# Heads with one difference and two products per halving, and feed-forward products over both parts of the operand at once

## The chip, the cores and the metric

The kernel runs on one core of a Trainium2 chip. The metric is the device time of one execution, in microseconds (us); the same program is executed several times and the median is compared. Matrices are float32 and every large product is made of three products of rounded parts, described below.

## The reference

Two blocks in a row on a sequence of 256 tokens, width 2048. Cut to what the change touches:

```python
# first block, end: feed-forward with a squared relu, 2048 -> 8192 -> 2048
h = x * (1.0 + sc2) + sh2
f = jnp.square(jax.nn.relu(h @ w_m1[l] + b_m1[l])) @ w_m2[l] + b_m2[l]
x = layer_norm(DEEPNORM_ALPHA * x + g2 * f, ln2_g[l], ln2_b[l])
...
# second block, layer 1: gated linear recurrence, 16 heads of 128, forward and backward
b = jnp.cumsum(fb, axis=2)                      # running sum of log forget gates
diff = b[:, :, :, None, :] - b[:, :, None, :, :]
decay = jnp.exp(jnp.where(lower_tri, diff, -jnp.inf))
scores = jnp.einsum("bhtk,bhsk,bhtsk->bhts", qb, kb, decay)
o_intra = jnp.einsum("bhts,bhsv->bhtv", scores, vb)
```

The first block has, ahead of the feed-forward, a modulation (`w_ada`), a wide input product, a long convolution by spectrum, a spatial gate and an output product; the second block has a convolution layer (31 taps) and then the recurrence. Their results are all needed in order, so the stages run one after the other.

## The kernel before

Activations lie transposed: 128 channels on the partitions, 256 tokens along the row; a matrix of width 2048 is 16 such tiles. A weight matrix comes from memory in "halves": [128, 8, 128] float32, 512 KB, eight 128x128 blocks for one output tile. There are 784 halves in one fixed list, `HALVES`, and all engines walk through it in step:

- SyncE (SP) fetches half h into one of four to six `ring` buffers when the half that lay there is done with.
- ScalarE (ACT) rounds it to `wh` (`hi(h)`, L1527), when TensorE is done with half h-4 (four `wh`/`wl` buffers).
- VectorE (DVE) makes the rest `wl = ring - wh` (`lo(h)`, L864). Both run three halves ahead of TensorE.
- TensorE (PE) does, for each of the eight blocks k, three matmuls of 256 columns into one PSUM tile: `wh` x high part, `wh` x low part, `wl` x high part of the operand (L503, L504, L505). The operand is split the same way: `Ah`, `Al` (16 tiles each) or `Bh`, `Bl` (32 tiles each).

**Feed-forward.** It is done in two passes (`fh` 0 and 1) over half of the hidden width. In each, 32 units of two halves (`H_M1`, operand A) give 32 hidden tiles, and then 16 units of four halves (`H_M2`, operand B) give a part of the 16 output tiles: 256 halves and 2048 blocks in all. Behind an `H_M1` unit ACT applies bias and relu out of PSUM into `tmpA` (L1734), DVE squares it (L1213), ACT rounds it to `Bh` (L1736), GpSimd (POOL) makes `Bl` (L1951). Behind an `H_M2` unit ACT scales (L1746, L1748) and DVE adds to the residual `XR` (L1146). In the first pass, DVE also adds one 512 KB piece of `w_ada` to a running sum after each `H_M1` unit (`add_chunk`, L883); these pieces come through two buffers (`ring` 4 and 5), and SP issues the fetch of one right behind the fetch of a weight half, once the piece two before it has been added (L429). At the end of the pass TensorE sums the last accumulator (`reduce_chunks(11)`, L515), before it goes on.

**Heads.** For each of 16 heads there are ten halves of `hgrn_w_in_2` (parts forget forward, forget backward, gate, query, value). "Tick" x is half x of this stage; each engine does its work on half x and then one step of each head under way. The head's work is cut into 22 steps over 22 ticks, so two or three heads overlap, and their work stands in the program of each engine between the halves (`HEAD_PLAN`). The decayed scores of 256x256 token pairs are made by recursive halving, for h = 128, 64, ..., 1 ("levels") and a diagonal:

- DVE makes, from the two running sums `ecum`, four 128-element differences (forward and backward, each for the left and the right side of a pair) into a 512-element tile `E` (L1405);
- ACT takes its exponential in one operation (L1891);
- POOL multiplies keys and query by it: four 128-element products into `Kp` and `Qp` (L2066);
- TensorE makes two 128x128 score products in plain float32 (L801), and DVE copies the right entries by a mask (L1414, `place`).

Behind the gate part (the third of the five), DVE scales both forget parts and the gate out of PSUM (L1464, L1468), ACT takes three sigmoids, and DVE makes forget gates and keys (L1478, L1480, L1485). When all levels of a head are placed, TensorE applies the scores to the values (L810); ACT squares and copies the result (L1896, L1899), TensorE sums it, ACT takes the root (L1697), DVE its reciprocal (L1432) and the normed, gated output (L1435, L1439). The transposes of the next head's values (L784) need the PSUM tile that L1899 copies from. Every engine works strictly in the order of its program; semaphores count what is done.

## Time and profile before

| | |
|---|---|
| runs of the kernel before | 2838.05 us median, 2837.49 to 2839.7 |
| the profiled execution | 2840.99 us, of which span 2838.9 us |
| PE busy | 2631.7 us (93%) |
| DVE busy | 1995.9 us (70%) |
| ACT busy | 1387.4 us (49%) |
| POOL busy | 744.8 us (26%) |
| TensorE clock, mean of the span | 0.971 of full |

Busy is the time in which an engine has at least one instruction under way; matmuls overlap each other, so a busy PE can still be slower than its peak. Idle time of an engine only matters where another waits for it. The feed-forward lies between about 881 and 1648 us of the span, the heads between about 2133 and 2758 us.

### The profile page before, as it was taken

To read this page: it belongs to the slowest core of one execution; us is meant where nothing else is said; L and a number is where in the kernel's file an instruction comes from. 1 tells how busy PE (TensorE), PEld (TensorE's weight loads), DVE (VectorE), ACT (ScalarE), POOL (GpSimd) and SP (SyncE) were. 2 spreads that over 40 slices of the span, in tenths; PEclk is the share of its full clock that TensorE was granted. 3 is DMA by queue.
4 is the path that set the end of the run, shared out by engine and by line. 5 is a ranking of instruction groups with operands and counts; after the bars stand their busy time and mean duration, and the time that the engine had idled before them with its cause. 6 is when DMAs were issued, how large, how long until landed. Compare 5 with 4: busy or idle time off the path is not lost.

```text
span 2838.9 us, 50831 instructions
## 1 busy us (share of the span) xinstructions
PE 2631.7 (93%) x20564; PEld 2561.0 (90%) x20564; DVE 1995.9 (70%) x2820; ACT 1387.4 (49%) x1946; POOL 744.8 (26%) x966
## 2 busy tenths in 40 slices
PE   4599998999998999999999989997899999999979
PEld 1499998999897999999999979987899999999979
DVE  7887665768656775444544469977658999999964
ACT  0243333344334453435543357766556666666652
POOL 1100000001101520001100018888003555555540
PEclk9799999999998999999999989999899999999999
DMA  8877654777763886555555525544354444444434
GB/s 319 347 262 249 227 201 151 255 265 253 263 215 129 274 270 200 181 185 183 182 184 175 176 82 179 180 142 139 104 171 156 139 137 141 142 149 140 137 101 152
DMA packets 146372, 535.13 MB, mean 188 GB/s; under 512 B 16632, under 2 KB 16793, under 8 KB 145689
## 3 DMA queue, kind: packets, MB, share of 16 engines
q1 hardware_dynamic: 143176, 520.33, 53.9%
q0 software_dynamic: 2960, 11.54, 1.2%
q8 instruction: 163, 2.67, 0.4%
q14 instruction: 73, 0.59, 0.1%
HBM read 525.51 MB, written 6.29 MB: 187 GB/s over the span
## 4 chain that ended last, share of the span: by engine, by line
PE 62%; DVE 19%; ACT 6%; POOL 5%; issue 4%; DMA 3%; SPq 0%; POOLq 0%; DVEq 0%; ACTq 0%
PE ps L503 19%; PE ps L504 18%; PE ps L505 18%; DVE wl L864 5%; DVE BF L1405 5%; POOL misc L2033 4%; PE ps L525 2%; DMA ring<-in_w_ada 2%; DVE AF L883 1%; ACT wh L1527 1%; DVE BF L1414 1%; PE ps L607 1%; PE ps L595 1%; PE ps L515 1%; DVE misc L1432 1%
## 5 line engine op out<-in xcount | busy, mean ns | idle before, releaser
L503 PE MATMUL ps<-Ah,wh 128*128 128x256 f32 x4480 | 1300.4, 290 | 22.3 <-DVE Al L868 13.7
L864 DVE TENSOR_TENSOR wl<-ring,wh 128x1024 fp32r<-128x1024 f32 x784 | 978.5, 1255 | 447.6 <-ACT wh L1527 445.7
L504 PE MATMUL ps<-Al,wh 128*128 128x256 f32 x4480 | 1275.3, 285 | 0.0
L505 PE MATMUL ps<-Ah,wl 128*128 128x256 f32 x4480 | 1275.1, 285 | 0.0
L1527 ACT CAST wh<-ring 128x1024 fp32r<-128x1024 f32 x784 | 816.6, 1043 | 454.7 <-PE ps L505 451.3
L503 PEld LDWEIGHTS ps<-Ah,wh 128*128 128x128 f32 x4480 | 867.5, 194 | 30.6 <-issue 17.6
L504 PEld LDWEIGHTS ps<-Al,wh 128*128 128x128 f32 x4480 | 868.2, 194 | 1.2
L505 PEld LDWEIGHTS ps<-Ah,wl 128*128 128x128 f32 x4480 | 867.1, 194 | 0.0
L504 PE MATMUL ps<-Bl,wh 128*128 128x256 f32 x1792 | 512.5, 286 | 0.0
L503 PE MATMUL ps<-Bh,wh 128*128 128x256 f32 x1536 | 444.6, 289 | 12.0 <-issue 7.0
L505 PE MATMUL ps<-Bh,wl 128*128 128x256 f32 x1536 | 437.6, 285 | 0.0
L504 PEld LDWEIGHTS ps<-Bl,wh 128*128 128x128 f32 x1792 | 349.6, 195 | 1.3
L2066 POOL TENSOR_TENSOR BF<-BF 128x128 f32<-128x128 f32 x512 | 278.9, 574 | 187.5 <-ACT BF L1891 164.2
L503 PEld LDWEIGHTS ps<-Bh,wh 128*128 128x128 f32 x1536 | 298.2, 194 | 13.3 <-issue 7.2
L505 PEld LDWEIGHTS ps<-Bh,wl 128*128 128x128 f32 x1536 | 298.0, 194 | 0.0
L2033 POOL TENSOR_TENSOR misc<-misc 128x256 f32<-128x256 f32 x224 | 234.5, 1047 | 41.4 <-ACT misc L1791 11.6
L1951 POOL TENSOR_TENSOR Bl<-tmpA,Bh 128x256 fp32r<-128x256 f32 x80 | 78.2, 978 | 544.7 <-ACT Bh L1736 468.4
L1405 DVE TENSOR_TENSOR BF<-misc 128x128 f32<-128x128 f32 x512 | 210.6, 470 | 3.8 <-POOL BF L2066 3.2
L1891 ACT ACTIVATE BF<-BF 128x512 f32<-128x512 f32 x128 | 81.0, 633 | 157.4 <-DVE BF L1405 157.2
L1791 ACT ACTIVATE misc<-misc,vec 128x256 f32<-128x256 f32 x240 | 110.8, 504 | 45.4 <-POOL misc L2033 41.1
L1951 POOL TENSOR_TENSOR Al<-tmpA,Ah 128x256 fp32r<-128x256 f32 x15 | 13.3, 887 | 392.6 <-ACT Ah L1769 226.5
L801 PE MATMUL ps<-BF 128*128 128x128 f32 x576 | 88.6, 277 | 21.7 <-DVE BF L1414 20.2
(211 smaller groups left out, 2306.2 us busy)
## 6 DMA issues: line engine op xcount, KB each, us to landing
ring<-in_w_m SPq DMA_DIRECT2D x256, 512.0 KB, 3.7
ring<-in_hgrn_w_in SPq DMA_DIRECT2D x160, 512.0 KB, 3.6
ring<-in_w_ada SPq DMA_DIRECT2D x144, 512.0 KB, 6.6
ring<-in_w_in SPq DMA_DIRECT2D x144, 512.0 KB, 4.6
ring<-in_conv_w_in SPq DMA_DIRECT2D x96, 512.0 KB, 3.6
AF<-in_w_ada SPq DMA_DIRECT2D x48, 512.0 KB, 8.8
ring<-in_w_ab SPq DMA_DIRECT2D x32, 512.0 KB, 4.8
ring<-in_w_o SPq DMA_DIRECT2D x32, 512.0 KB, 4.2
```

What stands on the lines that cost most here:

```text
L503: e.matmul(dst, hi[:, k, :], xh, start=first and k == 0, stop=False)
L504: e.matmul(dst, hi[:, k, :], xl, start=False, stop=False)
L505: done = e.matmul(dst, lo[:, k, :], xh, start=False, stop=last and k == 7)
L801: done = e.matmul(ps[b][:, a * P:a * P + P], Ku[:, a * P:a * P + P], Qu[:, x * P:x * P + P], start=True, stop=True)
L864: e.tensor_tensor(low[:], ring[SLOT[h]][:], hi[:].bitcast(F32), ALU.subtract).then_inc(s.lo, 1)
L1405: e.tensor_tensor(Ev[:, k, :, a, :], a0, a1, ALU.subtract).then_inc(dif, 1)
L1527: e.copy(wh[h % NSPLIT][:], ring[SLOT[h]][:]).then_inc(s.hi, 1)
L1791: prod.up(e.activation(dst, cp[:, j:j + 256], ACT.Copy, scale=col("conv_dw_2", 16 * j + n)))
L1891: e.activation(E[(step - 1) % 2], E[(step - 1) % 2], ACT.Exp).then_inc((s.exp0, s.exp1)[u], 1)
L1951: e.tensor_tensor(low, src, hi.bitcast(F32), ALU.subtract).then_inc(signal, 1)
L2033: padd.up(e.tensor_tensor(pa, pa, ptmp[padd.n % NTMP], ALU.add))
L2066: e.tensor_tensor(pairs(dst, h)[:, :, a, :], pairs(src, h)[:, :, a, :], Ev[:, k, :, a, :], ALU.mult).then_inc(kq, 1)
```

## The change

Two independent edits.

**Feed-forward.** The high and low parts of an operand become one tensor, `A2` and `B2`, with the low part as a second row block; `Ah`, `Al`, `Bh`, `Bl` are views of them. In `wide_half` a block takes two matmuls: `wh` x (high, low) with 512 columns into a whole PSUM bank, and `wl` x high with 256 columns into its lower half. The sum over `wh` x low so stands apart in the upper half and has to be added afterwards: ACT reads the upper half (with the bias; now without relu), DVE adds the lower half (one operation more), and then takes max and square in one. Behind `H_M2` DVE has one operation more as well.

**Heads.** DVE's four differences of a level become one 512-element difference; its sign is the same on both sides of a pair, so ACT takes two exponentials of 256 elements with the signs -1 and +1. POOL's four products become two of 256 elements, one for `Kp`, one for `Qp`; the latter walks the two sides backwards.

```diff
+        def wide_half(h, pb, both, ready, first, last):
+            hi, lo = wh[h % NSPLIT], wl[h % NSPLIT]
+            w.wait_ge(s.lo, h + 1)
+            for k in range(8):
+                ready(k)
+                xs = both(k)
+                e.matmul(pb.rearrange("p (a t) -> p a t", a=2), hi[:, k, :], xs, start=first and k == 0,
+                         stop=False)
+                done = e.matmul(pb[:, 0:256], lo[:, k, :], xs[:, 0, :], start=False, stop=last and k == 7)
+            done.then_inc(s.mm, 1)
...
                 w.wait_ge(s.rel, 32 * fh + n + 1)
-                rsq.up(e.tensor_tensor(x[:], x[:], x[:], ALU.mult))
+                e.tensor_tensor(x[:], pb[:, 0:256], x[:], ALU.add).then_inc(s.rad, 1)
+                w.wait_ge(s.rad, 32 * fh + n + 1)
+                rsq.up(e.scalar_tensor_tensor(x[:], x[:], 0.0, x[:], ALU.max, ALU.mult))
...
-                residual(n, 1.0 if fh else ALPHA, s.m2e, 16 * fh + n + 1)
+                w.wait_ge(s.m2e, 16 * fh + n + 1)
+                e.scalar_tensor_tensor(XR[:, n, :], XR[:, n, :], 1.0 if fh else ALPHA, tmpA[n % 4][:], ALU.mult,
+                                       ALU.add).then_inc(s.xa, 1)
+                w.wait_ge(s.xa, 16 * fh + n + 1)
+                e.scalar_tensor_tensor(XR[:, n, :], pb[:, 0:256], mod[:, 80 + n:81 + n], XR[:, n, :], ALU.mult,
+                                       ALU.add).then_inc(s.xr, 1)
...
-                for k in range(2):
-                    inc = pairs(ecum[u][k][:, 1 - k:257 - k], h)
-                    ref = ecum[u][k][:, h:h + 2 * h * (nb - 1) + 1:2 * h] if nb > 1 else ecum[u][k][:, h:h + 1]
-                    ref = ref.unsqueeze(2).to_broadcast([P, nb, h])
-                    for a in range(2):
-                        a0, a1 = (ref, inc[:, :, a, :]) if a == 0 else (inc[:, :, a, :], ref)
-                        e.tensor_tensor(Ev[:, k, :, a, :], a0, a1, ALU.subtract).then_inc(dif, 1)
+                o = 2200 + 520 * u
+                inc = strided(misc, o + 1, (259, 2), (2 * h, nb), (1, 2 * h))
+                ref = strided(misc, o + h, (260, 2), (2 * h, nb), (0, 2 * h))
+                e.tensor_tensor(E[li % 2].rearrange("p (k n h) -> p k n h", k=2, h=2 * h), inc, ref,
+                                ALU.subtract).then_inc(dif, 1)
...
-                    e.activation(E[(step - 1) % 2], E[(step - 1) % 2], ACT.Exp).then_inc((s.exp0, s.exp1)[u], 1)
+                    for a in range(2):
+                        side = E[(step - 1) % 2].rearrange("p (k n s h) -> p k n s h", k=2, s=2, h=h)[:, :, :, a, :]
+                        e.activation(side, side, ACT.Exp, scale=2.0 * a - 1.0).then_inc((s.exp0, s.exp1)[u], 1)
...
-                        for dst, src, k, a in ((Kp[x], kk[0], 0, 0), (Kp[x], kk[1], 1, 1),
-                                               (Qp[x], q, 1, 0), (Qp[x], q, 0, 1)):
-                            e.tensor_tensor(pairs(dst, h)[:, :, a, :], pairs(src, h)[:, :, a, :], Ev[:, k, :, a, :],
-                                            ALU.mult).then_inc(kq, 1)
+                        e.tensor_tensor(sides(BF, at(u, 10 + x), h, h), sides(BF, at(u, 1), h, 256 + h),
+                                        sides(BF, ev, h, 256 + h), ALU.mult).then_inc(kq, 1)
+                        e.tensor_tensor(sides(BF, at(u, 13 + x) + h, h, -h), sides(BF, at(u, 0) + h, h, -h),
+                                        sides(BF, ev + h, h, 256 - h), ALU.mult).then_inc(kq, 1)
```

TensorE in the feed-forward, two blocks of an `H_M1` half before, and two after (the lines are those of each program):

```order
L503 MATMUL ps<-Ah,wh 128x256
L504 MATMUL ps<-Al,wh 128x256
L505 MATMUL ps<-Ah,wl 128x256
L503 MATMUL ps<-Ah,wh 128x256
L504 MATMUL ps<-Al,wh 128x256
L505 MATMUL ps<-Ah,wl 128x256
```

```order
L522 MATMUL ps<-A,wh 128x512
L524 MATMUL ps<-A,wl 128x256
L522 MATMUL ps<-A,wh 128x512
L524 MATMUL ps<-A,wl 128x256
```

The columns are the same, 768 for a block; one matmul, and the weight load in front of it, is gone.

VectorE in the first pass, behind an `H_M1` unit before and after: the rests of two weight halves (`wl`), the square, and the piece of `w_ada` (`misc<-ring,cnd,misc`):

```order
L864 TENSOR_TENSOR wl<-ring,wh 128x1024 x2
L1213 TENSOR_TENSOR tmpA<-tmpA 128x256
L883 SCALAR_TENSOR_TENSOR misc<-ring,cnd,misc 128x1024
L864 TENSOR_TENSOR wl<-ring,wh 128x1024 x2
L1213 TENSOR_TENSOR tmpA<-tmpA 128x256
L883 SCALAR_TENSOR_TENSOR misc<-ring,cnd,misc 128x1024
```

```order
L882 TENSOR_TENSOR wl<-ring,wh 128x1024 x2
L1231 TENSOR_TENSOR tmpA<-ps,tmpA 128x256
L1233 SCALAR_TENSOR_TENSOR tmpA<-tmpA 128x256
L901 SCALAR_TENSOR_TENSOR misc<-ring,cnd,misc 128x1024
L882 TENSOR_TENSOR wl<-ring,wh 128x1024 x2
L1231 TENSOR_TENSOR tmpA<-ps,tmpA 128x256
L1233 SCALAR_TENSOR_TENSOR tmpA<-tmpA 128x256
L901 SCALAR_TENSOR_TENSOR misc<-ring,cnd,misc 128x1024
```

One operation more stands between the end of a unit and the piece of `w_ada`.

VectorE in the heads, a stretch of four ticks before and after: `BF<-misc` is the difference of a level, `BF<-masks,ps` a placed score:

```order
L864 TENSOR_TENSOR wl<-ring,wh 128x1024
L1414 COPY_PREDICATED BF<-masks,ps 128x256
L1405 TENSOR_TENSOR BF<-misc 128x8x16 x4
L864 TENSOR_TENSOR wl<-ring,wh 128x1024
L1405 TENSOR_TENSOR BF<-misc 128x16x8 x4
L864 TENSOR_TENSOR wl<-ring,wh 128x1024
L1405 TENSOR_TENSOR BF<-misc 128x32x4 x4
L864 TENSOR_TENSOR wl<-ring,wh 128x1024
L1414 COPY_PREDICATED BF<-masks,ps 128x256
L1405 TENSOR_TENSOR BF<-misc 128x64x2 x4
```

```order
L882 TENSOR_TENSOR wl<-ring,wh 128x1024
L1436 COPY_PREDICATED BF<-masks,ps 128x256
L1426 TENSOR_TENSOR BF<-misc 128x512
L882 TENSOR_TENSOR wl<-ring,wh 128x1024
L1426 TENSOR_TENSOR BF<-misc 128x512
L882 TENSOR_TENSOR wl<-ring,wh 128x1024
L1426 TENSOR_TENSOR BF<-misc 128x512
L882 TENSOR_TENSOR wl<-ring,wh 128x1024
L1436 COPY_PREDICATED BF<-masks,ps 128x256
L1426 TENSOR_TENSOR BF<-misc 128x512
```

Nothing changes its place; each group of four has become one operation of four times the length.

## Rows read from the trace of the kernel before

**Rows 1.** Stretches: length, busy of PE, PEld, DVE, ACT, POOL, PEclk, DMA, GB/s.
```profile
901.80:1062.00 160.20, 160.20 (x1339) 160.20 (x1338) 118.70 (x111) 79.06 (x110) 62.51 (x41) 1.00 0.82 273
1274.00:1460.00 186.00, 186.00 (x1552) 186.00 (x1551) 92.62 (x97) 93.12 (x129) 23.64 (x32) 1.00 0.55 182
...
2178.33:2213.28 34.95, 34.64 (x292) 34.41 (x291) 33.82 (x66) 24.62 (x33) 19.17 (x34) 1.00 0.46 154
2249.02:2286.69 37.67, 34.71 (x290) 34.31 (x289) 35.17 (x66) 25.03 (x33) 20.30 (x35) 1.00 0.43 143
```

**Rows 2.** TensorE in order of time at 1200 and at 893 us (us, us).
```profile
1200.35 0.28 PE L503 MATMUL ps<-Bh,wh 128*128 128x256 f32 x1
1200.47 0.28 PE L504 MATMUL ps<-Bl,wh 128*128 128x256 f32 x1
...
893.10 0.42 PE L504 MATMUL ps<-Al,wh 128*128 128x256 f32 x1
893.31 0.42 PE L505 MATMUL ps<-Ah,wl 128*128 128x256 f32 x1
```

**Rows 3.** The same, plain float32, 256 columns; three starts between are left out.
```profile
505.77 0.59 PE L607 MATMUL ps<-misc 128*128 128x256 f32 x2
...
506.63 0.59 PE L607 MATMUL ps<-misc 128*128 128x256 f32 x2
```

**Rows 4.** SyncE's queue in order of time, a fetch for `add_chunk`.
```profile
1056.09 0.43 SPq L429 DMA_DIRECT2D ring<-in_w_ada  x1
```

**Rows 5.** VectorE in order of time, the piece fetched in rows 4.
```profile
1062.78 1.28 DVE L883 SCALAR_TENSOR_TENSOR misc<-ring,cnd,misc 128x1024 f32<-128x1024 f32 x1 [0.18 <-DMA ring<-in_w_ada]
```

**Rows 6.** Waits of the first `H_M1` pass (us in total, times, longest).
```profile
DVE misc L883 <- DMA ring<-in_w_ada: 15.2, 21, 1.8
```

**Rows 7.** TensorE in order of time: where it stood idle (in brackets, and for whom).
```profile
1082.35 3.39 PE L515 MATMUL ps<-ones,misc 128*128 128x1 f32 x16 [3.44 <-DVE misc L883]
...
2260.70 0.68 PE L801 MATMUL ps<-BF 128*128 128x128 f32 x4 [1.44 <-DVE BF L1414]
...
2279.51 0.41 PE L784 MATMUL ps<-ident,misc 128*128 128x128 f32 x2 [1.52 <-ACT misc L1899]
...
2723.86 0.55 PE L503 MATMUL ps<-Bh,wh 128*128 128x256 f32 x1 [6.99 <-issue]
```

**Rows 8.** Groups of one head period, 2249.02 to 2286.69 (busy us, mean ns, idle before).
```profile
L2066 POOL TENSOR_TENSOR BF<-BF 128x128 f32<-128x128 f32 x32 | 17.3, 569 | 11.2 <-ACT BF L1891 10.1 <-PE ps L801 1.1
L1405 DVE TENSOR_TENSOR BF<-misc 128x128 f32<-128x128 f32 x32 | 13.4, 476 | 0.0
L864 DVE TENSOR_TENSOR wl<-ring,wh 128x1024 fp32r<-128x1024 f32 x11 | 13.3, 1213 | 0.0
...
L1891 ACT ACTIVATE BF<-BF 128x512 f32<-128x512 f32 x8 | 5.1, 632 | 9.9 <-DVE BF L1405 9.9
...
L2059 POOL TENSOR_TENSOR BF<-BF 128x256 f32<-128x256 f32 x1 | 0.8, 792 | 0.0
...
L1464 DVE TENSOR_TENSOR misc<-ps,statb 128x512 f32<-128x512 f32 x1 | 0.7, 676 | 0.0
...
L1439 DVE TENSOR_TENSOR misc<-misc 128x256 f32<-128x256 f32 x1 | 0.4, 424 | 0.0
```

**Rows 9.** VectorE in order of time, heads.
```profile
2253.59 0.41 DVE L1478 TENSOR_SCALAR misc<-misc 128x256 f32<-128x256 f32 x1 [2.33 <-ACT misc L1929]
...
2260.12 0.43 DVE L1414 COPY_PREDICATED BF<-masks,ps 128x256 f32<-128x256 uint8 x1
...
2718.21 0.89 DVE L1405 TENSOR_TENSOR BF<-misc 128x128 f32<-128x128 f32 x4
```

**Rows 10.** ScalarE in order of time, the exponential ahead of L1899.
```profile
2277.25 0.64 ACT L1891 ACTIVATE BF<-BF 128x512 f32<-128x512 f32 x1 [1.18 <-DVE BF L1405]
```

**Rows 11.** One line, L1927: one table load in each head but the first.
```profile
L1927 ACT ACT_TABLE_LOAD  x15: 1283/1283/1283, 2178.3 to 2703.1; - x15
```

**Rows 12.** One line, L2066 (ns min/median/max), all levels and heads.
```profile
L2066 POOL TENSOR_TENSOR BF<-BF x512: 450/520/2316, 2156.4 to 2746.5; 128x128 f32<-128x128 f32 x171
```

More of the change, by code:

```diff
@@ L180 @@
     "ablo gy mx woe gp "
-    "lg rel rsq m2e x2a x2v pq "
+    "lg rel rad rsq m2e xa x2a x2v pq "
     "sigb cpad prod padd tap ta cy sgz sz silu gz "
@@ L237, in _build @@
     wl = [sb(f"wl{i}", [P, 8, P], F32R) for i in range(NSPLIT)]
-    with nc.sbuf_tensor("Ah", [P, 16, T], F32R) as Ah, nc.sbuf_tensor("Al", [P, 16, T], F32R) as Al:
+    with nc.sbuf_tensor("A", [P, 2, 16, T], F32R) as A2:
         pass
     AF = sb("AF", [P, 2, 4096])
-    with nc.sbuf_tensor("Bh", [P, 32, T], F32R) as Bh, nc.sbuf_tensor("Bl", [P, 32, T], F32R) as Bl:
+    with nc.sbuf_tensor("B", [P, 2, 32, T], F32R) as B2:
         pass
@@ L257, in _build @@
     ps = [ctx.enter_context(nc.psum_tensor(f"ps{i}", [P, 512], F32)) for i in range(8)]
+    Ah, Al, Bh, Bl = A2[:, 0], A2[:, 1], B2[:, 0], B2[:, 1]
     kscr = nc.dram_tensor("kscr", [2, 4, P, 1024], F32, kind="Internal").ap()
@@ L347, in head_tiles, with strided, sides, at @@
         return q, kk, V, A, E, Kp, Qp
-    def pairs(ap, h):
-        return ap.rearrange("p (n s h) -> p n s h", s=2, h=h)
-    def pairs2(ap, h):
-        return ap.rearrange("p (k n s h) -> p k n s h", k=2, s=2, h=h)
+    def strided(tile, offset, *dims):
+        whole = tile[:]
+        return bass.AP(tensor=whole.tensor, offset=offset, ap=[list(whole.ap[0])] + [list(x) for x in dims])
+    def sides(tile, offset, h, pitch):
+        return strided(tile, offset, (pitch, 2), (2 * h, T // (2 * h)), (1, h))
+    def at(u, i):
+        return 256 * ((16 if u == 0 else 48) + i)
     n_ada = {16: 4, 32: 5, 48: 6, 64: 7}
@@ L373, in _build @@
         for n in range(32):
-            MAIN.append((s.rel, 32 * half + n + 1))
+            MAIN.append((s.rad, 32 * half + n + 1))
             if half == 0 and n == 16:
@@ L379, in _build @@
         for n in range(16):
-            MAIN.append((s.m2e, 16 * half + n + 1))
+            MAIN.append((s.xr, 16 + 16 * half + n + 1))
     ns, na, nz = 0, 0, 0
@@ L705, in tensor_program @@
             for n in range(32):
-                pb = bank()[:, 0:256]
+                pb = bank()[:]
                 for part in range(2):
-                    half(H_M1[fh] + 2 * n + part, pb, a_tiles(part),
-                         lambda k: wait_lo(w, 8 * part + k, 1), part == 0, part == 1)
+                    wide_half(H_M1[fh] + 2 * n + part, pb, lambda k: A2[:, :, 8 * part + k, :],
+                              lambda k: wait_lo(w, 8 * part + k, 1), part == 0, part == 1)
                     if part == 0 and fh == 0 and n == 16:
@@ L714, in tensor_program @@
             for n in range(16):
-                pb = bank()[:, 0:256]
+                pb = bank()[:]
                 for q in range(4):
-                    half(H_M2[fh] + 4 * n + q, pb, b_tiles(8 * q),
-                         lambda k: w.wait_ge(s.blo, 21 + 32 * fh + 8 * q + k + 1), q == 0, q == 3)
+                    wide_half(H_M2[fh] + 4 * n + q, pb, lambda k: B2[:, :, 8 * q + k, :],
+                              lambda k: w.wait_ge(s.blo, 21 + 32 * fh + 8 * q + k + 1), q == 0, q == 3)
                     if q == 0 and fh and n:
@@ L790, in head @@
                     if HALVINGS[li]:
-                        w.wait_ge(kq, 33 * t + 4 * li + 4)
+                        w.wait_ge(kq, 17 * t + 2 * li + 2)
                     else:
-                        w.wait_ge(kq, 33 * t + 33)
+                        w.wait_ge(kq, 17 * t + 17)
                         w.wait_ge(s.qq, hd + 1)
@@ L1205, in vector_program @@
             for n in range(32):
-                bank()
+                pb = bank()
                 for part in range(2):
@@ L1220, in vector_program @@
             for n in range(16):
-                bank()
+                pb = bank()
                 for q in range(4):
@@ L1471, in vector_program @@
                     if t:
-                        w.wait_ge((s.kq0, s.kq1)[u], 33 * t - 5)
+                        w.wait_ge((s.kq0, s.kq1)[u], 17 * t - 3)
                         w.wait_ge((s.cum0, s.cum1)[u], 2 * t)
@@ L1481, in vector_program @@
                     if t:
-                        w.wait_ge((s.kq0, s.kq1)[u], 33 * t)
+                        w.wait_ge((s.kq0, s.kq1)[u], 17 * t)
                     for k in range(2):
@@ L1728, in scalar_program @@
             for n in range(32):
-                pb = bank()[:, 0:256]
+                pb = bank()[:, 256:512]
                 for part in range(2):
@@ L1737, in scalar_program @@
             for n in range(16):
-                pb = bank()[:, 0:256]
+                pb = bank()[:, 256:512]
                 for q in range(4):
```

14 lines of the change are left out of this document (7 added, 7 removed).

## The prediction

> **What bounds the kernel now.** I read the stretches first, to see stage by stage which engine is full. In the feed-forward TensorE has no idle time: 160.20 of 160.20 us in the first pass's `H_M1`, 186.00 of 186.00 in the second's, and VectorE has half to three quarters of the time [rows 1]. "Busy" does not say whether it runs at its peak, so I then read single matmuls in order of time. With the granted clock at 1.0 (2.4 GHz) the 256-column matmuls start every 0.120 us, though 256 columns at that clock are 0.107; at half the clock they start every 0.21 us, which is just 256 columns at 1.2 GHz [rows 2]. So at full clock something costs each of them 13 ns that it does not at half clock. In the heads it is different: a period (one head, ten halves) takes 37.67 us, TensorE is busy for 34.71 and VectorE for 35.17 [rows 1], and VectorE is idle only while it waits 2.33 us for the sigmoids [rows 9]. 35.17 + 2.33 = 37.5: VectorE sets the period. What it does there is 13.4 us of differences and 13.3 us of weight rests [rows 8], and ScalarE waits 9.9 us per period for the differences.
>
> **Feed-forward: the products.** There are 2048 blocks. Each goes from three matmuls, 3 x 0.120 = 0.360 us, to one of 512 and one of 256 columns. A 512-column matmul on rounded parts is not in the trace. The nearest are plain float32 matmuls: each record streams its 256 columns twice, 512 column times, behind one weight load, and they start every (506.63 - 505.77) / 4 = 0.215 us [rows 3]. Only 2 ns over 512 columns at 2.4 GHz (0.213), so with one weight load per 512 columns the extra 13 ns is gone. I read this as: one load per 256 columns is just too much to hide, one per 512 is not. The block then takes 0.215 + 0.120 = 0.335; I take 0.336, 24 ns less. Bounds: if the 13 ns is a price per matmul whatever its length, 0.227 + 0.120 = 0.347, 13 ns less; if it is a lower column rate of rounded operands, 0.240 + 0.120 = 0.360, nothing. 2048 x 0.024 = **49 us** (between 0 and 51).
> The Trainium skill, "TensorE: Matmul & The Clock Gate", section "Back-to-back issue gap", gives N/2.4 + 2.5 ns for a matmul at full clock, with weight loads hidden. By it, as an estimate, the block goes from 3 x 109.2 = 328 to 216 + 109 = 325 ns, 5 us in all: a rule that speaks against this edit. The 0.215 of rows 3 agrees with it, the 0.120 of rows 2 does not, and the measurement decides.
>
> **Feed-forward: what stands around them.** VectorE gets one operation of 0.42 us per unit (as L1439 in [rows 8]) in 96 units. It has room in three of the four parts: at 92.62 of 186.00 us busy [rows 1] it goes to about 60%. It is exposed only where TensorE waits for the last unit of a stage: at the end of the first `H_M1` pass, where it now waits 3.44 us for the last piece of `w_ada` [rows 7], and at the end of the last `H_M2`. 2 x 0.42 = 0.9 us lost.
> The tight place is the first `H_M1` pass. VectorE is at 118.70 of 160.20 us, 4.27 per unit of 5.76; it gets 0.42 more while the unit shrinks to 16 x 0.336 = 5.38, 87% of the time. The pieces of `w_ada` come through two buffers: fetch issued at 1056.09, piece taken at 1062.78 on landing, 6.7 us [rows 4, 5]; then 1.28 for adding, 2 x 1.21 for the weight rests [rows 8], 0.4 until SyncE issues again: 10.8 us for two units, 5.4 per unit. VectorE already waits for these pieces 21 times, 15.2 us in all [rows 6]. The loop just meets the new 5.38, and with 7% more traffic than 273 GB/s the landing gets no quicker. I take 5.5 for the unit, 0.12 x 32 = 4 us lost. What bears it meanwhile is the lead of three halves; without it each late piece would stop TensorE. Feed-forward: 49 - 4 - 1 = **-44 us**.
>
> **Heads: VectorE, ScalarE, POOL.** Per level VectorE goes from four differences, 13.4 / 8 = 1.68 us, to one of 512 elements. The nearest row is the 512-element subtraction's like, L1464, at 0.676 [rows 8]. With POOL quiet the four took only 0.89 [rows 9], so half of the 1.68 is waiting for POOL. The new one costs from 0.68 up to 0.68 + 0.57 (one POOL operation ahead of it [rows 8]). VectorE's period falls from 35.17 to between 27.2 and 31.8 us. The skill's "SBUF — State Buffer", section "SBUF: two separate sides", names the cause: an exclusive port that the two share for a whole instruction. Four short ones meeting four short ones is by that the worst case; the trace agrees (1.68 against 0.89).
> ScalarE gets two exponentials of half the length for one of 0.632: 0.17 us more per level if a half takes 0.40, 1.4 per period, 25.03 to 26.4 [rows 1, 8]. POOL's four products (17.3 us per period) become two of 256 elements. The nearest is L2059, 0.792 [rows 8]: 16 x 0.79 = 12.7 us. All three are then below TensorE's 34.7.
>
> **Heads: what TensorE then waits for.** It has two stalls per period: 1.44 us for a placed score and 1.52 us for L1899 [rows 7]; each is some 0.16 longer by the run-out of the matmuls counted as busy. So the floor is 37.67 - 3.3 = 34.4. The second stall goes: L1899 is late since ScalarE stood 1.18 us for a difference just ahead of it [rows 10], and is a tick behind altogether. The first stays mostly. VectorE gets the sigmoids at 2253.59 and places the score at 2260.12 [rows 9]; between them are forget gates, keys, a weight rest, the reciprocal and the norm, 6.5 us, and not one difference. Ahead of 2253.59 stands ScalarE's row of four table loads and five activations, which begins when TensorE ends a half, not when VectorE is done. Starting half a microsecond earlier, with 0.2 for the longer exponential, leaves 1.1 of 1.6 us. A head period: 34.4 + 1.1 = 35.5, 2.2 us less (between 1.6, if ScalarE doesn't start earlier, and 3.3). The second head's period, 34.95 us with VectorE at 33.82 [rows 1], has no reciprocal in it yet: that TensorE can run at this pace is seen. From 2178.3 to 2703.1 there are 14 periods, mean 37.49 [rows 11]; with the second at 34.95 the other 13 take 37.68. 13 x 2.2 = 28.6, 0.4 in the second. At the end TensorE stands 6.99 us [rows 7] for a PSUM bank that VectorE reads behind three levels of the last head: 3 x 0.7 = 2 us less; and the last head's own levels, with nothing to cover them, some 2 us. Heads: **-33 us** (between 25 and 50).
>
> **Sum.** -44 - 33 = -77 us. The profiled execution took 2840.99, 3 over the median of the runs, 2838.05; the difference carries over: 2838 - 77 = **2761 us**. Under 0.2% (6 us) this measurement can't tell from no change.
>
> **Rivals.**
> *A, the above*, 0.43.
> *B, 13 ns per matmul whatever its length.* For: plain float32 streams in one instruction stay together, rounded ones need not. Against: rows 3 show 2 ns. Feed-forward 27 - 2 (the pieces of `w_ada` keep up at 5.55) = 25; 2838 - 58 = 2780. 0.2.
> *C, the column rate of rounded operands is 256 in 0.120 us*, or what the skill's rule says: the block keeps its time within 3 ns. For: half the clock hides the extra completely, as a fixed rate of fetching would. Feed-forward +1; 2838 - 32 = 2806. 0.2.
> *D, the heads don't gain*: the period stays with another engine. POOL's new products walk three dimensions, one of them backwards; none such is in the trace. At 16 products, with 3.1 us of other work, POOL reaches 37.7 us at 2.16 us a product, 2.7 times L2059. Against: over all levels the present products take 0.45 at the least and 0.52 in the median [rows 12], so the run length hardly counts. Then 2838 - 44 = 2794. 0.1.
> *E, slower*: a 512-column matmul of rounded parts isn't streamed once but taken like plain float32, in twice the column times: 0.427 + 0.120 = 0.547 per block, 2048 x 0.187 = +383, 2838 + 383 - 33 = 3188. It decides from a 512-column matmul of 0.256 us on (33 us over 2048 blocks). Against: the 256-column one shows nothing of it. 0.04.
> 0.03 is left for heads that gain all 50 with the feed-forward full: 2740.
>
> **Range.** 2741 to 2809 takes in A with its bounds (2741 to 2775), B, D and C at its value; outside are E and the edges of C and A, 0.18. Faster 0.95, same 0.01, slower 0.04.
>
> **What would show it.** Right: starts in the feed-forward 0.215 and 0.120 apart; its 256 halves 2.69 us each but in the first `H_M1` pass; a head period of 35 to 36 us with VectorE below 32 busy, the stall for L1899 gone and the one for the placed score still there. Wrong: 0.227 (B) or 0.240 (C) behind the 512-column matmul; waits of TensorE for `wl` in the first pass, which would say that the pieces of `w_ada` bound it; POOL above 30 us in a period (D); a longer wait ahead of L1478, if the two exponentials delay the sigmoids.

## The result and the profile after

| | before | after |
|---|---|---|
| runs, median (lowest to highest) | 2838.88 us (2837.49 to 2844.74) | 2789.56 us (2785.27 to 2794.57) |
| profiled execution, span | 2838.9 us | 2788.8 us |
| instructions of TensorE, VectorE, ScalarE, POOL | 20564, 2820, 1946, 966 | 18516, 2532, 2074, 710 |

The ratio is 0.9823, 95% interval 0.9801 to 0.9845: 49 us faster, where 77 were forecast. Marks that both programs have divide the difference: the first `H_M1` activation of ScalarE, its last `H_M2` activation (L1746 before, L1768 after), and in the heads the first sigmoid of each of the 16 heads (L1927 before, L1952 after), of which the first and the last are taken:

| stretch | before | after | difference | forecast |
|---|---|---|---|---|
| start to the first `H_M1` activation | 898.6 | 893.3 | -5.3 | 0 |
| from there to the last `H_M2` activation | 748.2 | 734.3 | -13.9 | -44 |
| first to last of these sigmoids, 15 head periods | 557.6 | 529.7 | -27.9 | -29 |
| behind it | | | -2.5 | -4 |

The first row is scatter: of what lies in front of that mark only the first unit's products and the place of the operand's parts in SBUF are changed, and over the profiles of all kernels it lies anywhere from 893 to 907 us. (The stretch between the feed-forward and the heads differs by 0.5.)

**Feed-forward.** TensorE in order of time (start, duration), in the first pass and at 1200 us:

```profile
919.70 0.39 PE L522 MATMUL ps<-A,wh 128*128 128x512 f32 x1
919.93 0.28 PE L524 MATMUL ps<-A,wl 128*128 128x256 f32 x1
920.05 0.39 PE L522 MATMUL ps<-A,wh 128*128 128x512 f32 x1
920.28 0.28 PE L524 MATMUL ps<-A,wl 128*128 128x256 f32 x1
...
1199.96 0.40 PE L522 MATMUL ps<-B,wh 128*128 128x512 f32 x1
1200.19 0.28 PE L524 MATMUL ps<-B,wl 128*128 128x256 f32 x1
1200.31 0.40 PE L522 MATMUL ps<-B,wh 128*128 128x512 f32 x1
```

The narrow matmul starts 0.230 behind the wide one, the wide one 0.117 behind the narrow one. Over a whole unit of 16 blocks that is 5.55 us, 0.347 a block, up to the sum in the first pass, and 5.65, 0.353 a block (0.236 and 0.117), from there to the first `H_M2` unit of the second pass; behind that it is 0.347 again (before: 5.76 for a unit, three times 0.120 [rows 2] for a block). The forecast had 0.336. Where TensorE stood, after the sum in mid-pass and at the end of the pass, and the stretch with the granted clock just behind the first of them (columns as in [rows 1]):

```profile
981.92 1.92 PE L533 MATMUL ps<-ones,misc 128*128 128x1 f32 x16 [1.40 <-DVE misc L901]
...
985.61 0.63 PE L522 MATMUL ps<-A,wh 128*128 128x512 f32 x1
986.03 0.41 PE L524 MATMUL ps<-A,wl 128*128 128x256 f32 x1
986.25 0.63 PE L522 MATMUL ps<-A,wh 128*128 128x512 f32 x1
...
1076.24 3.01 PE L533 MATMUL ps<-ones,misc 128*128 128x1 f32 x16 [3.15 <-DVE misc L901]
```

```profile
984.75:987.90 3.15, 3.15 (x11) 2.71 (x10) 0.43 (x1) 0.00 (x0) 0.00 (x0) 0.50 0.82 209
```

The first wait is new (before, the unit with the sum took 7.54 us without a wait, now 10.55). Behind it the clock is at 0.50 for some 3 us, and there a block is 0.42 + 0.22 = 0.64 us: just 768 columns at 1.2 GHz, nothing on top. At the full clock 768 columns are 0.320, and 0.027 to 0.033 is on top. The last piece of `w_ada` still keeps the end of the pass waiting, 3.15 for 3.44 [rows 7]. VectorE's waits for those pieces in the pass (us, times, longest) hardly grew against [rows 6]:

```profile
DVE misc L901 <- DMA ring<-in_w_ada: 17.8, 24, 1.3
```

In the second pass VectorE has 57% of the time, 60% were forecast [rows 1]:

```profile
1276.00:1460.00 184.00, 184.00 (x1043) 159.48 (x1042) 104.88 (x128) 92.65 (x127) 22.48 (x31) 1.00 0.59 187
```

**Heads.** The period is 35.60 us in all but the first two (37.68 before). First a stretch of ten periods (columns as in [rows 1]), then their groups on VectorE and POOL there (busy, mean ns, idle ahead):

```profile
2272.00:2627.00 355.00, 344.27 (x2874) 341.98 (x2873) 330.89 (x411) 259.35 (x410) 216.44 (x190) 1.00 0.49 149
```

```profile
L882 DVE TENSOR_TENSOR wl<-ring,wh 128x1024 fp32r<-128x1024 f32 x100 | 157.3, 1573 | 0.0
L1426 DVE TENSOR_TENSOR BF<-misc 128x512 f32<-128x512 f32 x80 | 77.7, 972 | 0.3
...
L1500 DVE TENSOR_SCALAR misc<-misc 128x256 f32<-128x256 f32 x20 | 12.4, 620 | 22.4 <-ACT misc L1954 22.4
```

```profile
L2089 POOL TENSOR_TENSOR BF<-BF 128x256 f32<-128x256 f32 x80 | 96.5, 1206 | 75.1 <-ACT BF L1916 64.8 <-PE ps L819 10.3
L2091 POOL TENSOR_TENSOR BF<-BF 128x256 f32<-128x256 f32 x80 | 92.8, 1160 | 0.0
```

The differences fell from 13.4 us a period [rows 8] to 7.8. But the weight rest, which the change doesn't touch, rose from 1213 to 1573 ns, ten times a period: 3.6 us given back. Each of the two products of a level takes 1.2 us, where the forecast took 0.79. One tick in order of time:

```profile
2243.16 0.90 DVE L1426 TENSOR_TENSOR BF<-misc 128x512 f32<-128x512 f32 x1
2243.47 1.19 POOL L2091 TENSOR_TENSOR BF<-BF 128x256 f32<-128x256 f32 x1
2243.98 1.75 DVE L882 TENSOR_TENSOR wl<-ring,wh 128x1024 fp32r<-128x1024 f32 x1
2244.96 1.38 POOL L2089 TENSOR_TENSOR BF<-BF 128x256 f32<-128x256 f32 x1 [0.30 <-ACT BF L1916]
...
2240.75 0.69 DVE L1426 TENSOR_TENSOR BF<-misc 128x512 f32<-128x512 f32 x1
2241.70 1.22 DVE L882 TENSOR_TENSOR wl<-ring,wh 128x1024 fp32r<-128x1024 f32 x1
2242.44 1.07 POOL L2089 TENSOR_TENSOR BF<-BF 128x256 f32<-128x256 f32 x1 [2.85 <-ACT BF L1916]
```

The rest at 2243.98 begins while a product still has 0.68 us to go, and takes 1.75; at 2241.70, with POOL idle for 0.7 us more, it takes 1.22. All 100 rests of the ten periods follow this: the 30 that begin with no product under way take 1.22 us, and the others are longer by what the product still has to go less 0.13 to 0.14 (0.34 us to go: 1.43; 0.67: 1.75; 0.79: 1.87). The difference takes 0.90 behind a product and 0.69 alone. Of TensorE's two stalls [rows 7] the one for L1899 (L1924 after) is gone and the one for the placed score is left:

```profile
2273.63 0.68 PE L819 MATMUL ps<-BF 128*128 128x128 f32 x4 [1.08 <-DVE BF L1436]
```

### The profile page after: what moved, and what is told of

It is laid out like the page before. It is cut to its first block, busy times and chain, and to the rows that moved or that the text cites. A ratio compares the mean times of both kernels' runs of the same rounds, so it can differ in the third digit from the quotient of the medians.

```text
span 2788.8 us, 46304 instructions
## 1 busy us (share of the span) xinstructions
PE 2609.9 (94%) x18516; PEld 2447.7 (88%) x18516; DVE 1998.8 (72%) x2532; ACT 1402.2 (50%) x2074; POOL 769.3 (28%) x710
## 4 chain that ended last, share of the span: by engine, by line
PE 65%; DVE 14%; issue 7%; ACT 6%; POOL 4%; DMA 4%; SPq 0%; POOLq 0%; DVEq 0%; ACTq 0%
PE ps L522 15%; PE ps L509 12%; PE ps L510 12%; PE ps L511 12%; PE ps L524 8%; DVE wl L882 4%; POOL misc L2058 4%; DMA ring<-in_w_ada 3%; PE ps L543 2%; DVE AF L901 1%; ACT wh L1549 1%; DVE BF L1436 1%; PE ps L625 1%; PE ps L613 1%; DVE BF L1426 1%
## 5 line engine op out<-in xcount | busy, mean ns | idle before, releaser
L509 PE MATMUL ps<-A,wh 128*128 128x256 f32 x3456 | 1006.6, 291 | 15.8 <-DVE A L886 9.2
L510 PE MATMUL ps<-A,wh 128*128 128x256 f32 x3456 | 983.8, 285 | 0.0
L511 PE MATMUL ps<-A,wl 128*128 128x256 f32 x3456 | 983.4, 285 | 0.0
L509 PEld LDWEIGHTS ps<-A,wh 128*128 128x128 f32 x3456 | 668.8, 194 | 21.1 <-issue 14.3
L510 PEld LDWEIGHTS ps<-A,wh 128*128 128x128 f32 x3456 | 669.4, 194 | 1.2
L511 PEld LDWEIGHTS ps<-A,wl 128*128 128x128 f32 x3456 | 668.6, 193 | 0.0
L522 PE MATMUL ps<-A,wh 128*128 128x512 f32 x1024 | 368.1, 403 | 7.7 <-DVE A L886 5.7
L522 PE MATMUL ps<-B,wh 128*128 128x512 f32 x1024 | 364.4, 400 | 0.0
L524 PE MATMUL ps<-A,wl 128*128 128x256 f32 x1024 | 290.4, 284 | 0.0
L524 PE MATMUL ps<-B,wl 128*128 128x256 f32 x1024 | 287.4, 281 | 0.0
L509 PE MATMUL ps<-B,wh 128*128 128x256 f32 x768 | 230.4, 300 | 19.1 <-DVE B L886 7.2
L522 PEld LDWEIGHTS ps<-A,wh 128*128 128x128 f32 x1024 | 195.1, 191 | 58.9 <-issue 4.9
L522 PEld LDWEIGHTS ps<-B,wh 128*128 128x128 f32 x1024 | 193.2, 189 | 46.0
L510 PE MATMUL ps<-B,wh 128*128 128x256 f32 x768 | 221.9, 289 | 0.0
L511 PE MATMUL ps<-B,wl 128*128 128x256 f32 x768 | 221.6, 289 | 0.0
L524 PEld LDWEIGHTS ps<-A,wl 128*128 128x128 f32 x1024 | 196.8, 192 | 0.0
L524 PEld LDWEIGHTS ps<-B,wl 128*128 128x128 f32 x1024 | 194.2, 190 | 0.4
```

What stands on the lines that cost most here:

```text
L509: e.matmul(dst, hi[:, k, :], xh, start=first and k == 0, stop=False)
L510: e.matmul(dst, hi[:, k, :], xl, start=False, stop=False)
L511: done = e.matmul(dst, lo[:, k, :], xh, start=False, stop=last and k == 7)
L522: e.matmul(pb.rearrange("p (a t) -> p a t", a=2), hi[:, k, :], xs, start=first and k == 0, stop=False)
L524: done = e.matmul(pb[:, 0:256], lo[:, k, :], xs[:, 0, :], start=False, stop=last and k == 7)
```

## The experiments

Twelve more kernels. Ratios are to the kernel before, run again beside them (its median was 2836 to 2841 us). The unit is the interval of `H_M1` units in the first pass ahead of the sum / behind it / in the second pass, the period that of the heads; both are read from the one profiled execution of each kernel.

| kernel | median us | ratio, 95% | unit us | period us |
|---|---|---|---|---|
| before | 2838.9 | | 5.76 / 5.76 / 5.76 | 37.68 |
| after | 2789.6 | 0.9823, 0.9801 to 0.9845 | 5.55 / 5.65 / 5.65 | 35.60 |
| x1_ff_only | 2823.0 | 0.9941, 0.9919 to 0.9962 | 5.55 / 5.65 / 5.55 | 37.68 |
| x2_heads_only | 2807.0 | 0.9894, 0.9871 to 0.9917 | 5.76 / 5.76 / 5.76 | 35.60 |
| x3_adjacent | 2791.4 | 0.9833, 0.9816 to 0.9849 | 5.55 / 5.55 / 5.55 | 35.60 |
| x4_wide_then_narrow | 2793.7 | 0.9836, 0.9816 to 0.9856 | 5.59 / 5.59 / 5.59 | 35.60 |
| x5_diff_only | 2806.1 | 0.9891, 0.9859 to 0.9923 | 5.55 / 5.55 / 5.65 | 36.8 |
| x6_place_first | 2798.0 | 0.9854, 0.9827 to 0.9880 | 5.65 / 5.55 / 5.55 | 36.20 |
| x7_reduce_later | 2780.1 | 0.9790, 0.9753 to 0.9826 | 5.65 / 5.65 / 5.55 | 35.60 |
| x8_best | 2790.7 | 0.9830, 0.9804 to 0.9856 | 5.65 / 5.65 / 5.55 | 36.20 |
| x9_tick6 | 2788.3 | 0.9823, 0.9801 to 0.9844 | 5.55 / 5.65 / 5.55 | 35.52 |
| x10_tick6_reduce | 2782.7 | 0.9790, 0.9777 to 0.9804 | 5.55 / 5.55 / 5.55 | 35.51 |
| y2_products_only | 2818.3 | 0.9933, 0.9911 to 0.9954 | 5.65 / 5.65 / 5.65 | 37.55 |
| y4_narrow128 | 3009.6 (one run) | | 7.31 / 7.31 / 7.31 | 35.60 |

### Each half of the change alone

x1_ff_only is the changed kernel with the heads of before, x2_heads_only the reverse (the diffs are those of the change, undone).

> Only the feed-forward edit; differences, exponentials and products of the heads as in the kernel before. If the two edits add up, this gains 12 to 17 us over the kernel before (the block at 0.353 instead of 0.360 us: 2048 x 0.0066 = 14 us, less the new stall in the first H_M1 pass) and the head period stays at 37.7 us. If the 5 us by which the changed kernel was ahead already before the feed-forward are part of the change, they show here too; if they are scatter of the fetches at the start, they need not.

> Only the head edit; the feed-forward as in the kernel before. Adding up: 29 to 32 us gained over the kernel before, head period 35.6 us, block in the feed-forward 0.360 us. The rival, that half of the heads' gain came from something that the feed-forward left behind (an earlier start of the fetches): a period clearly above 35.6.

The feed-forward is worth 16 us alone, the heads 32: together 48 of the 49. Within their intervals of some 6 us each way the halves add up. The unit with the sum is not a fixed cost of either kernel: with the feed-forward of before TensorE waited there 0 us (before) and 0.59 (x2_heads_only, a unit of 9.85), and with the changed one, where the sum is left in its place and the narrow matmuls are whole, 0 (x6_place_first) to 2.77 (x1_ff_only), units of 7.57 to 13.35.

### Why a block isn't 0.336

Two reasons were put against the flat price: that the gap between the two parts in SBUF costs the wide matmul something, and that what costs is the narrow neighbour.

x3_adjacent lays the high and the low part of each tile side by side:

```diff
+    A3 = A2[:].rearrange("p a k t -> p (a k t)").rearrange("p (k a t) -> p k a t", k=16, a=2)
...
-                    wide_half(H_M1[fh] + 2 * n + part, pb, lambda k: A2[:, :, 8 * part + k, :],
+                    wide_half(H_M1[fh] + 2 * n + part, pb, lambda k: A3[:, 8 * part + k, :, :],
```

> The changed kernel, but in the feed-forward the low part of a tile lies right behind its high part, so that the 512 columns are read in one run of 2 KB instead of two runs 16 or 32 KB apart. Theory 'gap': the jump in the moving operand costs the 7 to 8 ns by which the 512-column matmul is at 0.2345 instead of 0.227 us after it; then the block is at 0.347 or less and the kernel gains 12 to 14 us over the changed one. Theory 'columns': the price belongs to the number of columns; then the spacing stays at 0.2345 and the time within 3 us of the changed kernel.

x4_wide_then_narrow makes in each half eight wide matmuls, then eight narrow ones:

```diff
...
-                done = e.matmul(pb[:, 0:256], lo[:, k, :], xs[:, 0, :], start=False, stop=last and k == 7)
+            for k in range(8):
+                done = e.matmul(pb[:, 0:256], lo[:, k, :], both(k)[:, 0, :], start=False, stop=last and k == 7)
```

> The changed kernel, but each weight half does its eight 512-column matmuls first and its eight 256-column ones behind them. Theory 'columns': 0.2345 between wide ones, 0.120 between narrow ones, time as the changed kernel. Theory 'neighbour' (the weight load for the wide one is squeezed into the shorter narrow one before it, and what is over is paid by either): between wide ones 0.215 as in plain float32, because the load is wholly hidden, and 0.120 between narrow ones; then 2048 x 0.019 = up to 39 us less than the changed kernel.

x3_adjacent takes the same time as the change. Its unit stays at 5.55 throughout, but so it does in x10_tick6_reduce, which has the gap, so that isn't the gap's doing. In x4_wide_then_narrow the wide ones follow each other (start, duration):

```profile
919.48 2.00 PE L521 MATMUL ps<-A,wh 128*128 128x512 f32 x8
921.32 1.12 PE L524 MATMUL ps<-A,wl 128*128 128x256 f32 x8
922.28 0.40 PE L521 MATMUL ps<-A,wh 128*128 128x512 f32 x1
```

(921.32 - 919.48) / 8 = 0.230 and (922.28 - 921.32) / 8 = 0.120: the same as when they alternate. Neither layout nor neighbour: the 512-column matmul has its 0.017 to 0.023 on top of 0.213 by itself. The theories 'gap' and 'neighbour' both fell.

y4_narrow128 asks what the 13 ns of a 256-column matmul are:

```diff
-                done = e.matmul(pb[:, 0:256], lo[:, k, :], xs[:, 0, :], start=False, stop=last and k == 7)
+                for c in (0, 128):
+                    done = e.matmul(pb[:, c:c + 128], lo[:, k, :], xs[:, 0, c:c + 128], start=False,
+                                    stop=c == 128 and last and k == 7)
```

> The changed kernel, in which each feed-forward product with the weights' low part is two matmuls of 128 columns instead of one of 256; the sums are the same. This is the price of one matmul by itself. Theory (a fixed 13 ns for each matmul beside its columns): a block of eight grows by 13 ns for each k-step, from 0.3467 to 0.360 us, the unit from 5.55 to 5.76. Rival (a matmul takes at least the 0.12 us of a 256-column one, as if its weights had to be brought in first): 0.227 + 2 x 0.12 = 0.467 us, unit 7.5 us. Second rival (time goes by columns alone, 0.45 to 0.47 ns each): no change, 5.55 to 5.65.

```profile
959.83 0.45 PE L522 MATMUL ps<-A,wh 128*128 128x512 f32 x1
960.11 0.33 PE L525 MATMUL ps<-A,wl 128*128 128x128 f32 x2
960.28 0.45 PE L522 MATMUL ps<-A,wh 128*128 128x512 f32 x1
960.57 0.33 PE L525 MATMUL ps<-A,wl 128*128 128x128 f32 x2
```

The unit is 7.31 us, a block 7.31 / 16 = 0.457 with the same columns as 0.347. So it isn't a fixed 13 ns each (5.76 us), and not columns alone: one more matmul, with a weight load of its own, costs 0.110 us. The forecast of the first rival is the one that came near (7.5 us). The rows don't show it as 0.12 for each narrow matmul, though. The wide one now starts its follower after 0.287, the first narrow one after 0.058, just its columns and 5 ns, and the second after 0.112; only the sum of the three is what the rival says. A lower bound shows more plainly where there are hardly any columns, in the sums over the pieces of `w_ada` (here those of x7_reduce_later), 16 matmuls of one column with a weight load each:

```profile
991.08 1.84 PE L533 MATMUL ps<-ones,misc 128*128 128x1 f32 x16
...
992.78 0.48 PE L522 MATMUL ps<-A,wh 128*128 128x512 f32 x1
```

Behind the first they start 0.112 us apart. 256 columns (0.107) lie just under that, which is the reading that the prediction had for them, but it covers only 5 of the 13 ns: 0.120 is still 8 above it, and no run shows why. The reading's other half, that nothing is left on top at 512 columns, is what the 0.230 refutes.

### What carries the heads

x5_diff_only keeps the change's difference and exponentials and takes POOL's four products of before:

```diff
-                        e.tensor_tensor(sides(BF, at(u, 10 + x), h, h), sides(BF, at(u, 1), h, 256 + h),
-                                        sides(BF, ev, h, 256 + h), ALU.mult).then_inc(kq, 1)
...
+                        for dst, src, k, a in ((Kp[x], kk[0], 0, 0), (Kp[x], kk[1], 1, 1),
+                                               (Qp[x], q, 1, 0), (Qp[x], q, 0, 1)):
```

y2_products_only is the reverse, the change's two products behind the four differences and the one exponential of before (L1405, L1891 of that program).

> The changed kernel, but POOL's products stay four of 128 elements per level as in the kernel before; one difference and two exponentials as changed. Theory 'VectorE set the period and TensorE sets it now': the period stays at 35.6 us, because the stall that is left has no product in it, and the time is within 3 us of the changed kernel. Theory 'lock': the weight rest of VectorE, which in the changed kernel takes up to 1.75 instead of 1.21 us behind one long product, is nearer to 1.2 to 1.5 here, at no gain. If the products carried part of the gain, the period is 36 us or more.

> The changed kernel with the two products per halving, but with the four differences and the one exponential of before. Together with the kernel that had one difference and four products (period 36.8 where before has 37.68 and the change 35.60) this splits the heads' gain. Theory, that the parts add up: 37.68 less the 1.2 us that the products were worth there, 36.5 us, some 14 us above the changed kernel (2803 to 2806 us). Rival, that VectorE sets the period while it has four differences to make, so that products off its queue bring nothing: 37.4 to 37.7 us, 2817 to 2825 us.

Against 37.68 the difference alone brings 0.9 us a period, the products alone 0.13, and both 2.08. So in x5_diff_only the theory that TensorE alone sets the period now fell, in y2_products_only the rival held, and the parts don't add up. VectorE's groups there (busy, mean ns, idle ahead) show why; below them POOL and VectorE of one period of x5_diff_only:

```profile
L1436 DVE TENSOR_TENSOR BF<-misc 128x128 f32<-128x128 f32 x300 | 124.7, 474 | 0.3
L888 DVE TENSOR_TENSOR wl<-ring,wh 128x1024 fp32r<-128x1024 f32 x95 | 115.2, 1213 | 0.0
```

```profile
L2092 POOL TENSOR_TENSOR BF<-BF 128x128 f32<-128x128 f32 x32 | 24.4, 801 | 3.1 <-ACT BF L1916 3.1
...
L882 DVE TENSOR_TENSOR wl<-ring,wh 128x1024 fp32r<-128x1024 f32 x10 | 13.8, 1379 | 0.0
...
L1426 DVE TENSOR_TENSOR BF<-misc 128x512 f32<-128x512 f32 x8 | 7.0, 876 | 3.2 <-POOL BF L2092 3.2
```

With the four differences VectorE stays full, whatever POOL does. With one difference it has room, but the four products now take 0.80 us each (0.57 before [rows 8]), and VectorE waits 3.2 us a period for POOL to free the tile that a difference is written to. The products are worth their 1.2 us only once the differences are out of the way. And in y2_products_only, with the same two products, the rest still takes 1213 ns: there the four short operations lie beside the product, and the rest begins when it is done:

```profile
2298.26 1.63 DVE L1436 TENSOR_TENSOR BF<-misc 128x128 f32<-128x128 f32 x4
2298.56 0.78 POOL L2097 TENSOR_TENSOR BF<-BF 128x256 f32<-128x256 f32 x1
2299.81 1.21 DVE L888 TENSOR_TENSOR wl<-ring,wh 128x1024 fp32r<-128x1024 f32 x1
```

### The stall that is left

In x6_place_first VectorE serves the younger head first in every tick, in x9_tick6 in the ticks 6, 16, 26, ... alone:

```diff
-            for hd, _ in HEAD_PLAN[tick]:
+            for hd, _ in reversed(HEAD_PLAN[tick]):
```

```diff
-            for hd, _ in HEAD_PLAN[tick]:
+            for hd, _ in HEAD_PLAN[tick][::-1 if tick % 10 == 6 else 1]:
```

> The changed kernel with one thing more: within a tick VectorE works on the younger head first, so that the placed score that TensorE waits for stands ahead of the older head's reciprocal, norm and gating (2.7 us). If the stall of 1.1 to 1.2 us per period is this chain alone, it goes, the period falls from 35.6 to 34.4 to 34.6 us, and the kernel gains 13 to 18 us over the changed one. Rival: the stall moves to another place of the tick (the older head's output is late, or the difference comes later), period 35 us or more.

> The changed kernel, in which VectorE serves the younger head ahead of the older one in the ticks 6, 16, 26, ... alone (with the younger head first in all ticks, the wait for a placed score had moved to the next tick and grown from 1.07 to 1.68 us). Theory: the wait of 1.07 us for the placed score in front of the score matmul of tick 6 goes, and no other tick gains one, because the other nine ticks keep their order: head period 34.4 to 34.6 us where it is 35.60 now, 13 to 16 us below the changed kernel, about 2775 us. Rival: the wait moves again, since the older head's place and difference come 1.8 us later behind the younger head's scans in that tick: period 35.0 or more, at most 8 us gained or a loss.

TensorE's wait in x6_place_first, and in x9_tick6:

```profile
2272.62 0.68 PE L819 MATMUL ps<-BF 128*128 128x128 f32 x4 [1.68 <-DVE BF L1436]
```

```profile
2293.89 0.41 PE L802 MATMUL ps<-ident,misc 128*128 128x128 f32 x2 [1.03 <-ACT misc L1924]
```

In x6_place_first the stall moved to the next tick's placed score and grew; the period went to 36.20. In x9_tick6 no wait for a placed score is left, but one of the same length for L1924 came in its place: 35.52 for 35.60, nothing in the time. My theory, that the period is what TensorE has to do plus this one stall, fell. In the ten-period stretch VectorE of x9_tick6 is as busy as after the change, and waits as long for the sigmoids (L1500 22.4 us in both):

```profile
2272.00:2627.00 355.00, 344.64 (x2881) 342.36 (x2880) 330.86 (x410) 258.49 (x411) 214.04 (x190) 1.00 0.49 149
```

33.1 + 2.24 = 35.3 of 35.5 us: VectorE's queue with its one wait is as long as the period, as it was before the change, and a stall of TensorE that is moved within it comes up elsewhere. x6_place_first says the same from the other side: its period is 0.6 us longer, TensorE's work is the same, the wait for the sigmoids is 2.24 again, and VectorE's busy time is 33.8 us a period, 0.6 more.

### The sum in mid-pass

x7_reduce_later asks for the first pass's sums later, the one in mid-pass by a unit, the one at its end by two halves; the other engines' programs follow:

```diff
-                    if part == 0 and fh == 0 and n == 16:
+                    if part == 0 and fh == 0 and n == 17:
                         reduce_chunks(10)
-            if fh == 0:
-                reduce_chunks(11)
...
+                    if q == 1 and fh == 0 and n == 0:
+                        reduce_chunks(11)
```

x8_best has this and the edit of x6_place_first, x10_tick6_reduce this and that of x9_tick6.

> The changed kernel, but the two sums over the pieces of w_ada in the first feed-forward pass stand later in TensorE's and VectorE's programs: the first behind the first half of unit 17 instead of 16, the second behind the second half of the first H_M2 unit instead of between the stages. If TensorE's stalls of 1.4 and 3.15 us there and the stretch at half clock behind each are as they look, this gains 5 to 9 us over the changed kernel. Rival: the pieces simply come too slowly, and the same wait is found one unit later: 2 us or less.

> Both of the two edits before this one on top of the changed kernel. If they are independent: 18 to 27 us below the changed kernel, some 2765 us.

> The same order of heads in the ticks 6, 16, ... together with the sum matmuls one unit later in the feed-forward's first half (unit 17, and behind the first unit of the second stage). Theory: the two act in different stages and add up: the interval at the sum 7.44 us where it is 10.55, the gap between the two stages 185 where it is 195, the head period of the kernel with tick 6 changed alone; about 9 us below that kernel, 2762 to 2767 us if its period is 34.5, 2780 if it is 35.6.

TensorE of x7_reduce_later at both sums, with no idle time ahead:

```profile
991.08 1.84 PE L533 MATMUL ps<-ones,misc 128*128 128x1 f32 x16
...
1080.49 1.84 PE L533 MATMUL ps<-ones,misc 128*128 128x1 f32 x16
```

The unit with the sum takes 7.44 us (7.34 in x10_tick6_reduce), and from the last `H_M1` unit of the first pass to the first of the second it is 184.9 instead of 194.9. Of these 10 us some 3 are the pace of the products, which is 0.347 a block there; the kernels that have this pace there too and leave the sum in its place take 191.2 to 193.1, so asking later is worth 6 to 8. Both kernels come to 0.979, 7 to 9 us below the change; the intervals overlap (to 0.9826 and 0.9804, the change from 0.9801), but the stretches say the same. x8_best loses it again with its period of 36.20. x7_reduce_later and x10_tick6_reduce are the fastest that were run.

## Why the prediction was right, and where not

The direction held and the time, 2789.6, lies in the range of 2741 to 2809; the predicted 2761 is 28 too low. All of it is in the feed-forward.

**The products, 49 us: mis-sized.** The step that failed is "with one weight load per 512 columns the extra 13 ns is gone", taken from the plain float32 matmuls at 0.215 [rows 3]. A 512-column matmul on rounded parts starts its follower after 0.230, in long stretches after 0.236. At 0.347 a block gains 13 ns, 27 us in all, which is rival B's price. From the sum in the first pass to the first `H_M2` unit of the second, in 1296 of the 2048 blocks, it was 0.353 and gained 7 ns: 8.3 us less. The wait in mid-pass with the half clock behind it took 3 more (10.55 - 7.54) and the first unit's start 1 (6.81 us for 5.75): 27 - 8.3 - 4 = 14.7; measured were 13.9, and 16 with that half alone. The last two terms are those of this one profile: in x1_ff_only the start costs nothing and the sum 5.8. The rows of plain float32 were the wrong neighbour: one record of 256 columns with one weight load takes 0.215 there, and that says nothing of a record of 512 columns of rounded parts. Rival B has the right price here for a wrong reason: by y4_narrow128 one more matmul costs 0.110 and not 0.013, so it isn't a price per matmul whatever its length. The rule of the Trainium skill that was weighed, "TensorE: Matmul & The Clock Gate", section "Back-to-back issue gap", N/2.4 + 2.5 ns, would have made the feed-forward gain 5 us. That is 9 to 11 less than measured; for rounded parts the 0.120 and 0.230 us measured at 256 and 512 columns decide, neither of which it gives (109 and 216 ns). The prediction left out that the section gives this rule for a matmul by itself. For a stream of weight loads and matmuls it has 131 ns at 512 columns, and no run here bears that out either.

**The first pass, 4 us for `w_ada`: wrong mechanism.** The unit was to be 5.5 us by the loop of the pieces. It was 5.55, but by the products: 16 x 0.347. The pieces made VectorE wait 17.8 us in place of 15.2 and TensorE only where it needs all of them, at the two sums. At the first of them 3 us came on top, with a stretch at half the clock behind it, and x7_reduce_later took the waits at both away by asking later. TensorE never waited for VectorE's extra operation within the pass, as said.

**Heads, 33 us: the size was right** (30 in the profile, 32 alone), and so were the period (35.60 for 35.5), the stall for L1899 that goes and the one for the placed score that stays, 1.08. **The step on VectorE was not:** it was to fall to "between 27.2 and 31.8" and leave TensorE as the bound. It is at 330.9 x 35.60 / 355 = 33.2 us a period. The differences came out within the forecast (7.8 us a period, between 5.4 and 10), but the rest, put at no change, became dearer by 0.36 us ten times, and with its wait VectorE still fills the period. The 33.2 are 2.0 below the 35.17 of [rows 1], the gain of 2.08. That the same 2.2 came out of TensorE's stalls was luck: they are the other side of the same period, as x9_tick6 shows. The second period, where 0.4 us were to be gained, grew by 0.7 (34.8 to 35.5 us between first sigmoids), and the first, for which nothing was forecast, shrank by 1.5. POOL's product was 1.2 us, 0.85 with VectorE idle beside it (at 2264.83 us), and not 0.79 as L2059 [rows 8]. At 216.4 x 35.60 / 355 = 21.7 us a period it didn't matter, so rival D was rightly far.

**The end**, 4 us forecast, gave 2.5: TensorE's 6.99 us [rows 7] became 5.36, which is 1.6 where 2 were forecast, and 0.9 is left for its own levels, where 2 were put.

Rivals: B's price held, and C's lay 7 ns off in the 1296 blocks at 0.353; for E, which begins at 0.256 us for the wide matmul, there is nothing.

The Trainium skill's "SBUF — State Buffer", section "SBUF: two separate sides", has VectorE and POOL lock each other out of a shared port for a whole instruction. The trace agrees nearly: the rest at 2243.98 is longer by 0.53 us where a product has 0.68 to go, and over 100 rests the product's remaining time comes back in full but for 0.13 to 0.14 us. The prediction used it only for the operations that the change merges, and forgot the neighbour that stays.

## What to carry to other kernels

Before merging instructions on an engine that shares its way to SBUF with another, look at every operation that will then lie beside the longer one, above all the unchanged ones: here they gave back 3.6 of 5.6 us. Take the price of a new matmul from one of the same operand type, since here 512 columns of rounded parts cost 14 to 20 ns more than the plain float32 matmul of 256 columns that was taken to last as long; and don't split a matmul of 256 columns: the same columns cost 0.110 us more. If a sum needs the last piece of a stream, look whether it can be asked for a unit later; here that took away every wait for it. When a stall is moved and comes up at the same length elsewhere, it was never the bound: look for the queue that is as long as the period.

## What was not expected of the hardware

- Matmuls of one column with a weight load each start 0.112 us apart, nearly as far as those of 256 columns (0.120), and one more matmul in a block of the same columns cost 0.110. At half the granted clock, 0.42 + 0.22 for 512 and 256 columns, columns alone are left; whether bringing in the weights is what bounds it fits this, but wasn't measured by itself.
- The 512-column matmul has two paces at a granted clock of 1.0, 0.230 and 0.236 us (5.55 and 5.65 us a unit). The pace changes only where other matmuls stood between two blocks, with TensorE idle there or not: in x6_place_first it went from 5.65 to 5.55 at the sum, where TensorE did not wait, and in every kernel with blocks of one wide and one narrow matmul it is the quicker one from the second `H_M2` unit of the second pass on, behind the first matmuls for the norm's sums. The change has 5.55 then 5.65, x10_tick6_reduce 5.55 throughout, y2_products_only 5.65 up to that point. Before the change the unit is 5.76 in all. What sets it stays open, and it is known for the profiled executions alone; over all 2048 blocks it would be worth 2048 x 0.0063 = 13 us.
- The first `H_M1` activation lies at 893 to 907 us over the profiles, with nearly the same program ahead of it. Single profiles should be compared by stretches, not by their end.
